# Weight blocks in another order, half sums of the first pieces, and the last norm's rows spread on chip

## The reference

```
mod = silu(c) @ w_cond + b_cond ; sh1, sc1, gt1, sh2, sc2, gt2 = split(mod, 6)
h   = layernorm(x) * (1 + sc1) + sh1
z   = h @ w_in        # q | k | v | gu | gv | ga (1024) | gg (1024)
attn (8 heads x 64, causal, ALiBi) ; sgu (spatial gating, 8 groups x 64)
out = (sigmoid(ga)*(attn @ w_attn_up) + sigmoid(gg)*(sgu @ w_gmlp_up)) @ w_out
x   = layernorm(alpha*x + (1+gt1)*out) * ln1_g + ln1_b
h   = layernorm(x) * (1 + sc2) + sh2
q   = h @ w_peer_q    # 8 heads x 2 halves x 128
s   = scores of each half against 128 keys ; top 16 of each, top 16 of the sums
p   = sum over 8*16 experts of g * gelu(h . peer_u[i]) * peer_v[i]
out = layernorm(alpha*x + (1+gt2)*p) * ln2_g + ln2_b
```

## Time and profile before

| | |
|---|---|
| median of three runs | 930.67 us |
| profiled execution, its own time | 928.75 us |
| its span | 927.0 us |
| TensorE busy | 780.8 us (84%) |
| VectorE busy | 607.6 us (66%) |
| GpSimd busy | 491.3 us (53%) |
| ScalarE busy | 193.2 us (21%) |
| DMA traffic | 338.48 MB, 365 GB/s over the span |
| of it gathers of peer rows | 268.47 MB |

### The profile page before, as it was taken

One profiled execution on the slowest core, in us unless ns is written; L12 is line 12 of the kernel. 1 busy time (PEld: TensorE's weight loads), 2 busy tenths in 40 slices (PEclk: granted clock), 3 DMA queues, 4 the chain that ended last, 5 costly groups with the idle time before them and its releaser, 6 DMA issues.

```text
span 927.0 us, 8441 instructions
## 1 busy us (share of the span) xinstructions
PE 780.8 (84%) x2726; PEld 452.5 (49%) x2726; DVE 607.6 (66%) x1367; ACT 193.2 (21%) x492; POOL 491.3 (53%) x529
## 2 busy tenths in 40 slices
PE   5999999999977779796978869796977869696974
PEld 4876578778634345353534425352534435352322
DVE  6326587225779865759585756748585765888556
ACT  1012122204032312212121204212121312213111
POOL 1000000000577677777777676777677677777670
PEclk8699999999999799898989899897989899897987
DMA  9999985591699999999999999999999999999994
GB/s 347 365 375 338 335 302 218 190 310 46 243 407 409 409 409 409 409 409 409 410 409 409 410 409 400 407 408 410 367 411 409 410 409 407 409 392 408 408 409 161
DMA packets 112283, 338.48 MB, mean 365 GB/s; under 512 B 9184, under 2 KB 20976, under 8 KB 112112
## 3 DMA queue, kind: packets, MB, share of 16 engines
q0 software_dynamic: 73728, 268.47, 72.9%
q1 hardware_dynamic: 35936, 67.11, 20.3%
q10 hardware_dynamic: 2576, 2.37, 0.8%
HBM read 336.87 MB, written 1.05 MB: 365 GB/s over the span
## 4 chain that ended last, share of the span: by engine, by line
PE 35%; POOL 28%; DMA 14%; issue 11%; DVE 10%; ACT 1%; SPq 0%; DVEq 0%; POOLq 0%; ACTq 0%
POOL ring L362 28%; PE bank L1215 14%; DMA ring<-in_peer_u_dram,small 13%; PE bank L1027 11%; PE bank L1020 3%; DVE ring L867 3%; PE bank L1146 2%; DMA ring<-in_w_cond_dram 2%; PE bank L1160 1%; DVE ln L638 1%; PE h_ps L993 1%; DVE small L814 1%; DVE small L811 1%; DVE small L812 1%; DVE small L813 0%
## 5 line engine op out<-in xcount | busy, mean ns | idle before, releaser
L867 DVE CUSTOM_DVE_ANT_0 ring<-ring,h_ps 128x1024 f32<-128x1024 f32 x256 | 312.0, 1221 | 181.5 <-DMA ring<-in_peer_u_dram,small 171.6
L362 POOL DMA_INDIRECT ring<-in_peer_u_dram,small x256 | 246.8, 964 | 273.7 <-DVE small L848 193.4
L1215 PE MATMUL bank<-ring,small 128*128 128x512 f32 x512 | 258.7, 670 | 116.2 <-ACT small L549 116.2
L362 POOL DMA_INDIRECT ring<-in_peer_v_dram,small x256 | 240.5, 939 | 99.8 <-issue 64.4
L1215 PEld LDWEIGHTS bank<-ring,small 128*128 128x128 f32 x512 | 109.4, 217 | 256.0 <-issue 256.0
L1215 PE MATMUL bank<-ring,h_sb 128*128 128x512 f32 x500 | 220.1, 599 | 6.2 <-ACT h_sb L549 6.2
L1215 PEld LDWEIGHTS bank<-ring,h_sb 128*128 128x128 f32 x500 | 94.8, 192 | 121.5 <-issue 121.5
L1027 PE MATMUL bank<-hT,ring 128*128 128x256 f32 x448 | 101.5, 387 | 1.1 <-ACT hT L418 1.1
L1027 PEld LDWEIGHTS bank<-hT,ring 128*128 128x128 f32 x448 | 85.9, 194 | 15.9 <-issue 4.4
L1179 PEld LDWEIGHTS bank<-hT,wpq 128*128 128x128 f32 x512 | 59.6, 192 | 7.2 <-issue 7.2
L1179 PE MATMUL bank<-hT,wpq 128*128 128x128 f32 x512 | 59.8, 275 | 0.0
(11 more groups left out here) (187 smaller groups left out, 547.5 us busy)
## 6 DMA issues: line engine op xcount, KB each, us to landing
ring<-in_w_cond_dram SPq DMA_DIRECT2D x10, 2048.0 KB, 13.9
ring<-in_w_in_dram SPq DMA_DIRECT2D x8, 2048.0 KB, 12.7
wpq<-in_w_peer_q_dram SPq DMA_DIRECT2D x8, 1024.0 KB, 12.9
ring<-in_w_cond_dram SPq DMA_DIRECT2D x4, 1024.0 KB, 14.5
ring<-in_w_out_dram SPq DMA_DIRECT2D x2, 2048.0 KB, 10.4
ring<-in_peer_u_dram,small POOLq DMA_INDIRECT x256, 8.6
ring<-in_peer_v_dram,small POOLq DMA_INDIRECT x256, 8.6
ring<-in_w_in_dram SPq DMA_DIRECT2D x2, 1024.0 KB, 15.7
```

The costliest lines, as they stand in the source:

```text
L362: nc.gpsimd.indirect_dma_start(out=dst[e], out_offset=None, in_=table[0], in_offset=bass.IndirectOffsetOnAxis(ap=idx[:, k:k + 1], axis=0)) ...
L867: V.tensor_tensor_reduce(u_ring[e], u_ring[e], h_ps[:], 1.0, 0.0, ALU.mult, ALU.add, acol[:, g, e:e + 1]).then_inc(dots_done, 1)
L1215: last = T.matmul(bank[ACC_BANKS[t][m]][:], diag_of(p, g)[:, e, :], v_ring[e][:, m * BLK:(m + 1) * BLK], start=False, stop=end, skip_group ...
```

## The change

Six edits, which belong together:

1. **Order and slots of the blocks.** `PLACES` replaces `STREAM`: cond blocks 0 and 2 come first, then the first four row chunks of in blocks 0 and 1, then cond blocks 1 and 3, then the other four chunks of in 0 and 1. Slots are named for each block, and a block waits for the block before it in its slot (`BEFORE`).
2. **First modulation in two parts.** After cond blocks 0 and 2 the chunks 0 to 3 of `hT` are made, after 1 and 3 the chunks 4 to 7. TensorE takes two row chunks of cond blocks 0 and 2 and none of 1 and 3, so VectorE's part is 6, 6, 8 and 8 row chunks where it was 6, 6, 6 and 7.
3. **Half sums.** Pieces 0 to 3 are each made in two parts of four chunks, in banks 0 to 3 (`half_piece`). The first parts lie before and between the cond columns of blocks 1 and 3.
4. **Later sums.** The transposes of spatial weights and keys come together after block 2. Four sums of cond blocks (4 to 7) stand before the heads, where five stood; block 8 is summed in head 0 and saved in head 1.
5. **Buffers.** The second tile's attention output and the first PEER search move from `wpq` to other places. The q weights of head 6 then wait for the first tile's merge only, and are loaded before those of head 5. The first `score` is issued before one group of `up`, not after it.
6. **ln2.** One row of ln2_g and of ln2_b is loaded (8 KiB in all) into `ln1` when that is free. TensorE spreads each over 128 partitions by two matmuls with a row of ones, and ScalarE copies the result to `ln2`. The sums of cond blocks 10 and 11 come after pair 3 on TensorE (they came after pair 5).

```diff
+PLACES = [(("c", 0), 0), (("c", 2), 1), (("in", 0), 2), (("in", 1), 3), (("c", 1), 0), (("c", 3), 1), (("in", 2), 0),
+          (("in", 3), 1), (("c", 4), 2), (("c", 5), 3), (("c", 6), 2), (("in", 4), 0), (("c", 7), 3), (("in", 5), 1),
+          (("c", 8), 2), (("in", 6), 0), (("c", 9), 3), (("in", 7), 1), (("c", 10), 2), (("in", 8), 0), (("c", 11), 3),
+          (("ug", 0), 2), (("ua", 0), 1), (("o", 0), 3), (("o", 1), 0)]
...
-TE_ROWS = {0: 2, 1: 2, 2: 2, 3: 1}
+TE_ROWS = {0: 2, 1: 0, 2: 2, 3: 0}
...
+                    if b == ("c", 3):
+                        for n in range(2):
+                            later = slot(("in", n)).rearrange("p (k n) -> p k n", k=KC)[:, KC // 2:KC, :]
+                            sp.dma_start(later, w_of["in"][:, KC // 2:KC, n * BLK:(n + 1) * BLK]).then_inc(w_arrived[SLOT[("in", n)]], 16)
-                if b == ("c", 4):
+                if b == ("c", 5):
                     sp.dma_start(cond[:].rearrange("p a n -> p (a n)"),
...
-            for h in range(HEADS):
+            for h in (0, 1, 2, 3, 4, 6, 5, 7):
...
                 if h == 6:
-                    sp.wait_ge(idx_ready, 1)
-                    sp.wait_ge(up_ready, 2 * KC // 2)
+                    sp.wait_ge(merged, 4)
...
-            sp.wait_ge(cond_sum, 12)
-            sp.dma_start(ln2[:, LN_G, :], ln2_g[0:1, :].broadcast_to([P, D])).then_inc(ln2_in, 16)
-            sp.dma_start(ln2[:, LN_B, :], ln2_b[0:1, :].broadcast_to([P, D])).then_inc(ln2_in, 16)
+            sp.wait_ge(h2_ready, 2 * TILES)
+            sp.dma_start(ln1[0:1, LN_G, :], ln2_g[0:1, :]).then_inc(ln2_in, 16)
+            sp.dma_start(ln1[0:1, LN_B, :], ln2_b[0:1, :]).then_inc(ln2_in, 16)
...
+            def save_ln2(i):
+
+                act.wait_ge(ln2_spread, 1 if i == LN_B else 2)
+                for m in range(2):
+                    nc.scalar.activation(ln2[:, i, m * BLK:(m + 1) * BLK], bank[4 + m][:], ACT.Copy).then_inc(ln2_saved, 1)
...
-            for i in range(1, HEADS // 2 - 1):
-                weigh(i, 0)
-                weigh(i, 1)
+            weigh(1, 0)
+            weigh(1, 1)
+            save_ln2(LN_B)
+            weigh(2, 0)
+            weigh(2, 1)
             weigh(HEADS // 2 - 1, 0)
+            save_ln2(LN_G)
...
             for r in (1, 3):
+                cond_block(r // 2)
+                cond_block(2 + r // 2)
+                dve.wait_ge(cond_sum, r + 1)
+                ks = slice(2 * r - 2, 2 * r + 2)
+                V.tensor_copy(mod1[:, 0, ks], bank[COND_BANK][:, ks]).then_inc(mod1_ready, 1)
...
-            cond_save(8)
...
-                if j == 3:
-                    cond_save(9)
+                if j in (1, 3):
+                    cond_save(8 + j // 2)
...
-                if i == HEADS // 2 - 1:
+                if i == 2:
                     cond_save(10)
                     cond_save(11)
...
+            HALVES = ((0, 2, 1, 3), (4, 6, 5, 7))
+
+            def half_piece(n, part):
...
+                if part == 0:
+                    pe.wait_ge(in_first[b], 16)
+                else:
+                    arrived(("in", b))
+                dst = bank[PIECE_BANKS[n]]
+                for m in range(2):
+                    col = (2 * half + m) * P
+                    for i, k in enumerate(HALVES[part]):
...
+            cond_columns(0)
+            cond_columns(2)
+            half_piece(0, 0)
+            half_piece(1, 0)
+            cond_columns(1)
+            half_piece(2, 0)
+            cond_columns(3)
+            half_piece(3, 0)
             for b in range(IN_GA):
-                piece(2 * b)
-                piece(2 * b + 1)
-                if b == 1:
+                if b < 2:
+                    half_piece(2 * b, 1)
+                    half_piece(2 * b + 1, 1)
+                else:
+                    piece(2 * b)
+                    piece(2 * b + 1)
+                if b == 2:
                     pe.wait_ge(spat_masked, 1)
-                    turn_weights(0)
-                    turn_weights(1)
-                if b == 2:
                     pe.wait_ge(keys_in, 16)
-                    for n in range(2, 6):
+                    for n in range(6):
                         turn_weights(n)
-                if b:
-                    cond_total(3 + b)
-            cond_total(3 + IN_GA)
+                if b >= 2:
+                    cond_total(2 + b)
+            cond_total(2 + IN_GA)
...
-                if j == 2:
-                    cond_total(9)
+                if j in (0, 2):
+                    cond_total(8 + j // 2)
...
-            up(1, [5])
             score(0)
-            up(1, [7] + list(range(8, 16)))
+            up(1, [5, 7] + list(range(8, 16)))
...
+            def spread_ln2(i):
+
+                for m in range(2):
+                    last = T.matmul(bank[4 + m][:], ones[0:1, :], ln1[0:1, i, m * BLK:(m + 1) * BLK], start=True, stop=True)
+                last.then_inc(ln2_spread, 1)
+
+            add_rows(2)
             pe.wait_ge(h2T_saved, 4)
+            pe.wait_ge(ln2_in, 32)
+            spread_ln2(LN_B)
+            add_rows(3)
+            pe.wait_ge(ln2_saved, 2)
             cond_total(10)
             cond_total(11)
-            add_rows(HEADS - 2)
+            add_rows(4)
+            add_rows(5)
             pe.wait_ge(cond_saved, 8)
+            spread_ln2(LN_G)
+            add_rows(6)
+            pe.wait_ge(ln2_saved, 4)
             clear(1)
```

More of the change, by code:

```diff
@@ L50 @@
 FAR = -1.0e30
[L53 to L57, removed]
+PLACES = [(("c", 0), 0), (("c", 2), 1), (("in", 0), 2), (("in", 1), 3), (("c", 1), 0), (("c", 3), 1), (("in", 2), 0),
[3 rows of a table added]
+STREAM = [b for b, _ in PLACES]
+SLOT = dict(PLACES)
+TURN = {b: sum(SLOT[e] == SLOT[b] for e in STREAM[:n]) for n, b in enumerate(STREAM)}
+BEFORE = {b: next((e for e in reversed(STREAM[:n]) if SLOT[e] == SLOT[b]), None) for n, b in enumerate(STREAM)}
+C_PLACE = {n: p for p, n in enumerate([0, 2, 1, 3, 4, 5, 6, 7, 8, 9, 10, 11])}
 IN_Q, IN_K, IN_V, IN_GU, IN_GV, IN_GA, IN_GG = 0, 1, 2, 3, 4, 5, 7
 PIECES = 18
-TE_ROWS = {0: 2, 1: 2, 2: 2, 3: 1}
+TE_ROWS = {0: 2, 1: 0, 2: 2, 3: 0}
 DVE_ROWS = (1, 3, 5)
@@ L131, in build @@
         attnT0 = small[:, 2048:2560].rearrange("p (c t) -> p c t", c=WC)
+        attnT1 = attnT0
         spat_nat = small[:, 2048:3072].rearrange("p (g s) -> p g s", s=P)
         def search(p):
-            part = wpq[:, 12288:13312] if p == 0 else small[:, 0:1024]
+            if p == 0:
+                sums = small[:, 1536:2048]
+                return small[:, 1024:1280], scratch[:, 512:768], sums[:, 0:256], sums[:, 256:512], sums
+            part = small[:, 0:1024]
             return part[:, 0:256], part[:, 256:512], part[:, 512:768], part[:, 768:1024], part[:, 512:1024]
@@ L174, in build @@
         bank += [h_ps[:, 0:BLK], h_ps[:, BLK:D]]
-        PIECE_BANKS = (0, 1)
+        PIECE_BANKS = (0, 1, 2, 3) + 7 * (0, 1)
         SCORE_BANKS = (2, 3)
@@ L195, in build @@
         w_arrived = [sem(f"w_arrived{i}") for i in range(SLOTS)]
-        c_first = {n: sem(f"c{n}_first") for n in (2, 3)}
-        in0_first = sem("in0_first")
+        c_first = {n: sem(f"c{n}_first") for n in (2, 1, 3)}
+        in_first = [sem(f"in{n}_first") for n in range(2)]
         ln1_in = sem("ln1_in")
         ln2_in = sem("ln2_in")
+        ln2_spread = sem("ln2_spread")
+        ln2_saved = sem("ln2_saved")
         wpq_in = [sem(f"wpq_in{i}") for i in range(2)]
@@ L273, in _ @@
             sp.dma_start(x_sb[:], x[0].rearrange("(t p) d -> p t d", p=P)).then_inc(x_in, 16)
-            for n, b in enumerate(STREAM):
+            for b in STREAM:
                 kind, i = b
-                if n >= SLOTS:
-                    old, j = STREAM[n - SLOTS]
+                if BEFORE[b] is not None:
+                    old, j = BEFORE[b]
                     if old == "c":
-                        sp.wait_ge(cacc_ready, j + 1)
-                        if j in TE_ROWS:
-                            sp.wait_ge(cond_sum, j + 1)
+                        sp.wait_ge(cacc_ready, C_PLACE[j] + 1)
+                        if TE_ROWS.get(j):
+                            sp.wait_ge(cond_sum, C_PLACE[j] + 1)
                     elif old == "in":
@@ L467, in _ @@
                 piece(n)
-                if n == 3:
-                    save_wT(0)
-                    save_wT(1)
                 if n == 5:
-                    for m in range(2, 6):
+                    for m in range(6):
                         save_wT(m)
@@ L942, in _ @@
                 dots(i, 1, 1)
-            dve.wait_ge(ln2_in, 32)
+            dve.wait_ge(ln2_saved, 4)
             dve.wait_ge(cond_saved, 8)
@@ L977, in cond_columns @@
                                  start=False, stop=False, skip_group_check=True)
-                pe.wait_ge(cacc_ready, n + 1)
+                pe.wait_ge(cacc_ready, place + 1)
                 for m in range(BLK // P):
                     k = n * (BLK // P) + m
```

(16 more changed lines are left out.)

53 lines of the change are left out of this document (28 added, 25 removed).

## The result

The changed kernel took 920.71 us (median of 5, 919.21 to 922.70), the kernel before 930.29 beside it (5 runs, 928.22 to 930.74). The ratio is 0.9905, 95% interval 0.989 to 0.992: 8.8 us or 0.95% faster, between 7.4 and 10.2. Forecast were 918.8 and a range of 915 to 925. The profiled execution has a span of 919.0 us (own time 920.71), 8.0 less than before.

What follows compares the result with a forecast made beforehand. TensorE work after the first modulation was taken to bound the front, DMA bytes the PEER gathers. Gathers 6.8 us earlier plus 5.1 for bytes made 11.9, from 930.67 to 918.8; range 915 to 925.

Steps and rivals of the forecast that it cites:

- The half sums: Front: half pieces start at 23.1 us, the first four pieces end at 55.2 instead of 63.3, 8.1 us gained.
- Head 0 to `up`: From 9.0 us gained at head 0, block 8's sum takes 1.05 and waits for VectorE's softmax 1.3, leaving 6.6.
- cover of ScalarE: Front: ScalarE, blocked by DMA issues, saves pieces 0 to 2 by 54.1; the fifth needs them at 55.2, cover 1.1 us.
- `score` earlier: Before the gathers: issuing `score` before a group of `up` gives 0.2 us.
- The first gather: End of the front: the gathers start 6.8 us earlier, near 232.5 us.
- The PEER stage: Gathers, bound by DMA bytes: 2.10 MB fewer at 409 GB/s save 5.1 us; bounds nothing and 7.4.
- head 6's: PEER stage: 1 MiB of q weights moves from beside head 7's to near 187 us, priced within the 2.10 MB at 409 GB/s.
- ln2's: PEER stage: two 512 KiB broadcasts, 1.05 MB, go, priced within the 2.10 MB at 409 GB/s.
- A: Rival, PEER stage: GpSimd's pace, not bytes, bounds the gathers, so only the front counts: 923.9 us; chance 0.11.
- B: Rival, front: cold clock, ScalarE's blocked saves or late cond block 8 eat 5 to 6 of 6.8: about 924.5; chance 0.14.
- C: Rival, PEER stage: slower, dry spells (DMA queue empties) multiply, 2.3 us each; six new ones give 932.6; chance 0.07.
- D: Rival, better: no VectorE waits and no dry spell (slow DMA stretches in 655 to 670 us): 915.2; chance 0.06.

Runs made afterwards that it cites:

- e2: Changed kernel with the first halves of pieces 0 to 3 moved behind the column sums of cond block 3: 934.18 us, ratio 1.0048 to the kernel before.
- e8: Changed kernel plus eight further 512 KiB broadcast loads (4.19 MB) in the gather stage: 930.39 us, ratio 1.0015 to the kernel before.
- e6: Changed kernel with ln2 broadcast from DRAM and head 6's q weights late, as before (front alone): 922.80 us, ratio 0.9938 to the kernel before.
- e7: Kernel before with ln2's rows spread on chip, head 6's weights early, `score` earlier and the buffers these need: 926.29 us, ratio 0.9968.
- e1: Changed kernel with ln2's rows broadcast from DRAM again: 921.77 us, ratio to the kernel before 0.9906 to 0.9933.
- e12: The changed kernel again, no edit: 920.35 us, ratio 0.9896 to the kernel before.
- e5: The changed kernel again, no edit: 920.73 us, ratio 0.9919 to the kernel before.
- e4: Changed kernel with head 6's q weights issued with head 7's, as before: 920.25 us, ratio to the kernel before 0.9882 to 0.9914.
- e11: Changed kernel with e9's dummy matmuls, and head 6's q weights loaded with head 7's: 921.47 us, ratio 0.9915 to the kernel before.
- e9: Changed kernel with dense 128x128 dummy matmuls on TensorE before the half sums: 921.90 us, ratio 0.9913 to the kernel before.

## Why the prediction was right, and where it was off

**The direction and the mechanisms held.** Half sums pull TensorE's work forward (e2: 12.4 to 13.5 us hang on them), bytes bound the gathers (e8), the parts add (e6, e7). Of the gain 11.9 was forecast and 8.8 measured (7.4 to 10.2). That the time came out only 1.9 above the forecast is in part luck of the base. I subtracted from 930.67, the median of three executions, and the kernel before runs in two groups: of its 42 executions beside e1 to e12, the 23 with a mean granted clock of 0.918 to 0.923 average 928.6 us, the 19 with 0.927 to 0.931 average 930.3, and my three (930.29 to 930.74) are like the second. From the 929.1 that is the median of the 42, the same gain would have given 917.2, some 3.3 below what was measured. The ratio over all runs is the better measure of the gain.

**The half sums: 8.1 forecast, 6.0 and 7.3 in two executions.** The four pieces' end was 55.2 in the forecast and is 57.5 in the profile, 56.2 in e5 (38.69 + 17.51); before, 63.5. One cause is in the start. I had taken block 0's columns at the full clock, as they are in the trace before, and block 2's at half. In the profiled execution block 0's ran at half as well, so block 2's ended at 24.8 for 22.0; and since SyncE's load of cond block 1 waits for block 0's columns, it was issued at 19.79 and not 17:

```profile
19.79 0.37 SPq L303 DMA_DIRECT2D ring<-in_w_cond_dram  x1
...
24.89 0.37 SPq L303 DMA_DIRECT2D ring<-in_w_cond_dram  x1
```

I had looked at the clock's level, but took its phase as fixed. That accounts for this execution: VectorE's sum of block 3 ends at 38.6, before TensorE asks for it at 39.17. The other cause binds in e5, with the start on time: VectorE was to begin block 3 at 30.8 and begins it at 31.72, when the data comes. The end of that sum in the changed kernel's profile, then its start in e5's:

```profile
33.15 5.47 DVE L656 SCALAR_TENSOR_TENSOR ln<-ring,c_col,ln 128x512 f32<-128x512 f32 x7
```

```profile
31.72 0.49 DVE L651 TENSOR_SCALAR ln<-ring,c_col 128x512 f32<-128x512 f32 x1 [0.80 <-DMA ring<-in_w_cond_dram]
```

TensorE waits 1.07 us for it, is through with block 3's columns at 38.69 where the forecast had 37.9, and the five half pieces behind take 17.5 for 17.3: the 1.0 us that e5 misses at 56.2. The clock's return was forecast well: the first two half pieces take 9.10 and 9.23 us, for 9.2 forecast; 32 such matmuls take 7.17 at the full level (the row at 106.72), so some 4 us ran at half, for 4.6.

**Head 0 to `up`: 2.35 forecast, 2.34 measured** (70.91 us before, 73.25 after). The sum of block 8 and two waits of 0.47 and 0.49, forecast 0.6 and 0.7, at the forecast places. This step held. So did the cover of ScalarE, by 1.6 us (1.0 in e5): its issues block it to 54.12, the third save ends at 55.7, the fifth piece starts at 57.33.

```profile
41.92 10.89 ACTq L436 DMA_DIRECT2D wpq<-in_b_spatial_dram  x2
...
54.12 1.08 ACT L461 ACTIVATE wpq<-bank 128x512 f32<-128x512 f32 x2 [12.68 <-PE bank L1061]
```

**`score` earlier: 0.2 forecast, -0.4 to -0.6 measured** (e7). The step missed what the moved work waits for.

**The first gather: 6.8 forecast, 4.1 and 4.7 in the traces, 4.2 in e12** (235.15, 234.49, 234.99 for 239.23); e6's trace has 5.4 (233.83), its timing 5.8.

**The PEER stage: 5.1 forecast, 3.0 timed (e7), of a kernel that also loses 0.4 to 0.6 ahead of it.** So the stage by itself gives near 3.5; the changed kernel's three traces have 3.9, 5.1 and 4.1 (687.8 us from the first gather to the end before, 683.9, 682.7 and 683.7 after). The term that failed is head 6's: "2.10 MB at 409 GB/s" priced its MiB as ln2's. ln2's bytes lie in a full stretch and returned 1.2 and 2.6 us. Head 6's lay beside the first 8 gathers, where DMA is below its rate without it, and returned -0.4 to 1.0. My own row showed it: the slice at 232 to 255 has 243 GB/s, and I read the limit from 240 on as if it began at once. A DMA share of 1.02 over 665 us says nothing of the first 10. The sizes of the two terms are known to about 1 us each; that head 6's is the smaller rests on three comparisons (e4, e6 against e1, e11) and on the windows.

**The rivals.** A is refuted by e8. B, the front eaten, is true in kind and under half in size: 1.0 (e6's timing) to 2.7 us (the first trace) of the 5 to 6 went, none through ScalarE. C did not show: behind the first 20 us of the stage, stretches of 5 us fall short of 409 GB/s by 3.9 us in sum in the changed kernel and by 4.1 in the kernel before. D's hope that the dry spell goes fell too: in the changed kernel it stands at 650 to 660, and another, near 825, stands in both kernels.

## What to carry to other kernels

Price bytes by what the DMA does in the very microseconds where they move: here a MiB beside the first gathers, where DMA moved 262 GB/s, was nearly free, and 4.19 MB in the middle, at 409, cost 8.9 to 9.7 us of the 10.3 by size. When an order of loads delays some input, measure what fills the gap: here the same order is 4.5 us slower than before without the half sums and 8.8 faster with them. And when moving work forward, look up what the moved instruction waits for as well as what it precedes.

## What the hardware showed that I had not expected

**The clock's phase varies.** Of eight profiled executions with the same start (the changed kernel, e1, e2, e4, e5, e6, e8, e12), block 0's sixteen one-column matmuls ran at the full level in five (1.95 to 2.04 us) and at half in three (3.57). The Trainium skill (TensorE: Matmul & The Clock Gate, "Part 1: The HAM clock gate") says that the number of slow matmuls differs from run to run of one kernel; the traces agree. In seven of them (e2 has no half pieces there) those start at 23.01 to 23.40 us after a full group and at 25.89 or 26.20 after a slow one.

**The clock's record can be wrong.** The windows of the changed kernel, then of e5, over the same stretch:

```profile
17.00:20.00 3.00, 3.00 (x16) 3.00 (x16) 2.89 (x4) 0.00 (x0) 0.00 (x0) 1.00 1.05 386
```

```profile
17.00:20.00 3.00, 3.00 (x17) 3.00 (x16) 2.88 (x4) 0.00 (x0) 0.00 (x0) 0.52 1.05 386
```

In both stretches TensorE ran at half: in the first the eight one-column matmuls at 17.85 take 1.85 us, for 1.03 at the full level (16.01 in e5), in the second the sixteen at 16.90 take 3.37, for 1.95. The first record claims 1.00, and it does so for all of 14 to 30 us. The durations decide.

**The half level without idleness.** In e9 TensorE was busy for 9.00 of the 9 us from 17 to 26 at a granted clock of 0.50. Before the fall it had run 7 us of dummies, the transposes and one group of one-column matmuls. Whether that group lets the clock fall, and by which property, the runs don't settle.
